# State part with the first Neumann matrices on GpSimd, and routed key chunks with products of 512 columns

## The chip, the core and the metric

The kernel runs on one core of a Trainium2 chip. A core has TensorE (matrix products into PSUM), VectorE, ScalarE and GpSimd (element-wise work), and SyncE, which issues the DMAs here. Each engine has its own queue and runs it in order; they wait for each other by semaphores. The metric is the time of one execution on the device in microseconds (us), the median of several. The profile is of one execution, and its own time stands beside the median below.

## What is computed

Two layers over 256 tokens of width 1024, all in float32. The first is an attention and pooling block with a gated FFN. The second is a Conformer-like convolution beside an RWKV-7 recurrence, followed by a PEER layer (product keys, 16,384 experts). The change touches the recurrence part and the PEER keys:

```python
def conformer_conv(p_conv, w_dw, b_dw, ln_w, ln_b):
    a, b = jnp.split(p_conv, 2, axis=-1)
    y = a * jax.nn.sigmoid(b)
    y = lax.conv_general_dilated(y, w_dw[:, None, :], ..., feature_group_count=CONV_CH) + b_dw   # 31 taps, 512 channels
    mu = jnp.mean(yf, axis=-1, keepdims=True)
    var = jnp.mean(jnp.square(yf - mu), axis=-1, keepdims=True)
    yf = (yf - mu) * lax.rsqrt(var + LN_EPS) * ln_w + ln_b
    return jax.nn.silu(yf)

def step(state, inp):                       # rwkv7_mix, scanned over 256 tokens, 8 heads of 64
    r_t, k_t, v_t, w_t, kk_t, a_t = inp
    sa = jnp.einsum('bhij,bhj->bhi', state, -kk_t)
    state = state * w_t + sa[..., None] * (kk_t * a_t) + v_t[..., None] * k_t
    y_t = jnp.einsum('bhij,bhj->bhi', state, r_t)
    return state, y_t

def chunk(xc):                              # peer_ffn
    ... the 16 best of 128 x 128 experts of each of 8 heads, gate = softmax(best)
    h = jax.nn.gelu(jnp.einsum('thkd,td->thk', ue, xc), approximate=False)
    return jnp.einsum('thk,thkd->td', (gate * h).astype(xc.dtype), ve)
```

## The kernel before

**Weights.** All weight matrices come as chunks of 128x1024 float32 (512 KB) through a ring of four slots (`RING`): SyncE loads `raw`, ScalarE writes its rounded copy `w_hi` (`split`, L497), and VectorE subtracts to get the rest, `w_lo` (`split`, L926). In the W_Q stage and the first chunks of the key table GpSimd does that subtraction (`lo_part`, L1540). The activations are split in the same way into `x_hi` and `x_lo`. TensorE then makes three products for each of 8 tiles of a chunk (`three`, L1576 to L1578: w_hi x_hi, w_hi x_lo, w_lo x_hi), 24 matmuls of 256 columns. `chunk_used` frees the ring slot.

**State part** (about 516 to 614 us). The recurrence is computed in four blocks of 64 tokens. First come the Gram products of the features (L1900), masked on VectorE (L1259, `gram_masked`); VectorE then adds the identity to the four masked matrices `DU` and so makes `R` (L1264, `neu_start`). Ten Neumann steps (list `NEUMANN`, products at L1920 to L1924, all 64x64) follow, each over four blocks, in one queue of 40 jobs on TensorE. A job waits until all results of the job three before it are evicted: by ScalarE (L771, `neu_act`) or by VectorE (`neu_dve`). A step's product that is evicted by ScalarE is a plain copy. Then come `m1` (L1938), `w1` (L1942), `m1T` (L1949), `m2` (L1955), `phi` (L1965), `u` (L1974 and L1975), the state chain of two steps (L1982, each with VectorE work between), `sa` (L1990) and the outputs `y` (L2008, L2022).

The 31-tap convolution runs beside it. Eleven taps are VectorE's own (`own_tap`, L1243, placed between its evictions). Twenty are made in 40 halves: ScalarE multiplies (`tap_pair`, L750, two operations of 128x256, into a buffer of three halves, so half m waits for the addition of half m - 3), and GpSimd adds each to `co` (L1565, 128x512). ScalarE makes 8 of the 40 ahead of the steps, 24 after evictions of the steps, 4 after `m1T` and 4 after `m2`. After the state chain, VectorE adds both sums (`conv_out`) and computes the bonus (`bonus_gate`); TensorE sums for the LayerNorm's mean (`ln_mean`, L1996) and variance (`ln_var`, L2013).

**Key table** (EXP_U, 128 chunks, 655 to 1126 us). From chunk 60 on (`DENSE_AT`) each chunk also does one of 64 groups of routing: VectorE makes one-hot matrices (`hots`, L1447), ScalarE multiplies gates in (`gates_in`, L856), TensorE makes `dense` products (L2071), VectorE multiplies them with stored activations (`mix`, L1459 and L1461; `late`, L1470). ScalarE applies gelu (`h_step`, L846 and L848). Key chunks use bank n % 4. **Value table** (EXP_V, 128 chunks, `v_step`, L2105): 512-column products, operands `f_hi`, `f_lo` (L1485) for the first chunk.

The order on each engine is the order in which the code is written; no scheduler moves it.

Of the kernel before, what the change touches and what calls it, by code (L numbers as in the profile page):

```python
# [26 lines left out]
P = 128  # L27
TOK = 256
# [113 lines left out]
ACT_TAPS = 20  # L142

# [27 lines left out]
def build(nc, ins, out):  # L171
    with ExitStack() as ctx:
# [17 lines left out]
        x_hi = sb("x_hi", [P, KT, TOK], F32R)  # L190
        x_lo = sb("x_lo", [P, KT, TOK], F32R)
# [201 lines left out]
        gT = i0T  # L393

# [91 lines left out]
        def _(act):  # L486
# [294 lines left out]
            while pair < 2 * ACT_TAPS - 4:  # L781
                tap_pair(pair)
                pair += 1
# [3 lines left out]
            while pair < 2 * ACT_TAPS:  # L787
                tap_pair(pair)
                pair += 1
# [5 lines left out]
            act.activation(rstd2, bank[1][:, 0:TOK], ACT.Sqrt, bias=V("eps", 1, 2), scale=1.0 / 512).then_inc(S("ln_std"), 1)  # L795
            for f in range(2):
                act.wait_ge(S("y_prod"), 2)
                act.activation(yy.rearrange("p f (t c s) -> p c f t s", t=2, c=2)[:, f], bank[4 * f][:, :].rearrange("p (f t s) -> p f t s", f=4, t=2),
                               ACT.Copy).then_inc(S("y_out"), 1)
# [39 lines left out]
            def h_step(n):  # L839

                if n <= DENSE_AT:
                    split(EXP_U + n + AHEAD)
                act.wait_ge(chunk_used, EXP_U + n + 1)
# [6 lines left out]
                if DENSE_AT <= n < NKEY - 1:  # L850
                    split(EXP_U + n + AHEAD + 1)
# [7 lines left out]
            for n in range(NKEY):  # L859
                if n == EXP_AT:  # L860
                    act.wait_ge(S("best_shifted"), 1)
                    act.activation(gate[:, :, :, :], gate[:, :, :, :], ACT.Exp).then_inc(S("gate_exp"), 1)
                if n == DENSE_AT:
                    act.wait_ge(S("gT"), 1)
# [3 lines left out]
                if n == NKEY - 1:  # L868
                    act.wait_ge(S("g_mixed"), GROUPS)
                    act.activation(by_four(f_hi[:, :]), h_chunk(0), ACT.Copy).then_inc(S("g_hi"), 1)  # L870
                h_step(n)
# [43 lines left out]
        def _(dve):  # L915
# [288 lines left out]
            dve.sem_inc(S("rk"), 1)  # L1204
# [9 lines left out]
            dve.sem_inc(S("factors"), 1)  # L1214
# [17 lines left out]
            dve.sem_inc(S("bonus_read"), 1)  # L1232
# [30 lines left out]
            for b in range(4):  # L1263
                dve.tensor_tensor(R_[:, b], DU[:, b], mask("eye64"), ALU.add).then_inc(S("neu_start"), 1)  # L1264
# [24 lines left out]

            for t in range(2):  # L1290
# [5 lines left out]

            for c in range(4):
# [4 lines left out]

            def decay_of(c):
# [6 lines left out]
            own.after(dve.memset(st[:, 0], 0.0))  # L1310

# [14 lines left out]
            dve.wait_ge(S("tap_added"), 2 * ACT_TAPS)  # L1326
            for f in range(2):
                v = slice(2 * f, 2 * f + 2)
                dve.wait_ge(S("own_taps"), 4 * (31 - ACT_TAPS))
                own.mark(dve.tensor_tensor(co[:, v], bank[6 + f][:, :].rearrange("p (a t) -> p a t", a=2), co[:, v], ALU.add))  # L1330
            own.wait()
            dve.sem_inc(S("conv_out"), 1)
            for f in range(4):
                bonus_gate(f)
            own.wait()
            dve.wait_ge(S("ln_mean"), 1)
            for f in range(4):
                dve.scalar_tensor_tensor(co[:, f], bank[1][:, 0:TOK], -1.0 / 512, co[:, f], ALU.mult, ALU.add).then_inc(S("ln_centred"), 1)
            for n in range(19, 22):
                split(MIX + n + AHEAD)  # L1340
# [4 lines left out]

            for f in range(2):
# [50 lines left out]
            dve.sem_inc(S("best_shifted"), 1)  # L1397
# [36 lines left out]
            dve.sem_inc(S("gate_done"), 1)  # L1434
# [4 lines left out]
            dve.tensor_copy(gT[:, :], bank[5][:, 0:TOK]).then_inc(S("gT"), 1)  # L1439
# [782 lines left out]
```

## Time and profile before

| | us |
|---|---|
| median of 3 runs (1490.42 to 1492.27) | 1491.6 |
| the profiled execution | 1492.93 |
| its span | 1491.1 |
| TensorE busy | 1419.8 (95%) |
| VectorE busy | 1043.9 (70%) |
| ScalarE busy | 824.2 (55%) |
| GpSimd busy | 190.4 (13%) |

Times are from the start of the span. PE is TensorE, PEld its weight load, DVE is VectorE, ACT is ScalarE, POOL is GpSimd.
### The profile page before, as it was taken

Reading aid. Unit: us, or ns where it says so; the run is one execution under the profiler, and the core shown is the slowest. Engines: PE = TensorE matmul, PEld = TensorE weight load, DVE = VectorE, ACT = ScalarE, POOL = GpSimd, SP = SyncE. Lnnn points to the kernel's source line nnn. Section 1 sums busy time; section 2 is a strip of 40 time slices with the busy share of each in tenths; the row PEclk is TensorE's granted clock in tenths of the full one; section 3 lists DMA queues with packets and bytes.
Section 4 is the critical chain, followed back from the end, with each engine's and each line's share of the span. In section 5 each row is a group of like instructions: output and inputs, shape, how many; then the busy total and the mean of one; then the engine's idle time right before and its main releaser. Section 6 shows DMA issues by size and latency. Waiting matters only on the chain.

```text
span 1491.1 us, 30993 instructions
## 1 busy us (share of the span) xinstructions
PE 1419.8 (95%) x11674; PEld 1328.9 (89%) x11674; DVE 1043.9 (70%) x1848; ACT 824.2 (55%) x1548; POOL 190.4 (13%) x108
## 2 busy tenths in 40 slices
PE   5999899999979987889999999999999999999997
PEld 5989889999969987889999999999998888888885
DVE  5478657878767685569973978889985555555554
ACT  6344546656547773545444567777765545544553
POOL 0030000000000272047884000000000000000000
PEclk9999999999999997999999999999999999999999
DMA  6547556667734300354555554444446555555551
GB/s 238 191 153 256 186 198 212 241 229 267 253 102 139 100 4 4 114 183 157 185 183 189 179 168 138 138 139 141 142 143 218 191 195 193 191 194 196 189 192 56
DMA packets 68372, 253.00 MB, mean 170 GB/s; under 512 B 7584, under 2 KB 7840, under 8 KB 67488
## 3 DMA queue, kind: packets, MB, share of 16 engines
q1 hardware_dynamic: 67104, 245.40, 48.5%
q10 hardware_dynamic: 1152, 5.98, 1.0%
q8 instruction: 82, 1.34, 0.4%
q14 instruction: 34, 0.28, 0.1%
HBM read 249.25 MB, written 2.10 MB: 169 GB/s over the span
## 4 chain that ended last, share of the span: by engine, by line
PE 89%; DVE 5%; ACT 3%; issue 2%; POOL 1%; DMA 0%; ACTq 0%; DVEq 0%; POOLq 0%
PE bank L2105 23%; PE bank L1576 18%; PE bank L1577 18%; PE bank L1578 18%; PE bank L2071 4%; PE bank L1924 1%; DVE arena L947 1%; POOL arena L1565 1%; PE bank L2056 0%; DVE arena L944 0%; PE bank L1619 0%; PE bank L1634 0%; DVE w_lo L926 0%; DMA vec<-in_vec 0%; PE bank L1843 0%
## 5 line engine op out<-in xcount | busy, mean ns | idle before, releaser
L1576 PE MATMUL bank<-x_hi,w_hi 128*128 128x256 f32 x2120 | 620.2, 293 | 17.9 <-DVE x_lo L957 6.3
L926 DVE TENSOR_TENSOR w_lo<-raw,w_hi 128x1024 fp32r<-128x1024 f32 x364 | 445.2, 1224 | 228.8 <-ACT w_hi L497 225.9
L1578 PE MATMUL bank<-x_hi,w_lo 128*128 128x256 f32 x2120 | 604.5, 285 | 0.0
L1577 PE MATMUL bank<-x_lo,w_hi 128*128 128x256 f32 x2120 | 604.5, 285 | 0.0
L497 ACT ACTIVATE w_hi<-raw 128x1024 fp32r<-128x1024 f32 x416 | 439.0, 1056 | 182.7 <-PE bank L2105 167.2
L1576 PEld LDWEIGHTS bank<-x_hi,w_hi 128*128 128x128 f32 x2120 | 411.1, 194 | 28.3 <-issue 20.7
L1577 PEld LDWEIGHTS bank<-x_lo,w_hi 128*128 128x128 f32 x2120 | 412.1, 194 | 0.4
L1578 PEld LDWEIGHTS bank<-x_hi,w_lo 128*128 128x128 f32 x2120 | 411.1, 194 | 0.0
L2105 PE MATMUL bank<-w_hi,x_lo 128*128 128x512 f32 x508 | 156.5, 389 | 0.0
L2105 PE MATMUL bank<-w_lo,x_hi 128*128 128x512 f32 x508 | 156.4, 389 | 0.0
L2105 PE MATMUL bank<-w_hi,x_hi 128*128 128x512 f32 x508 | 156.3, 389 | 0.0
L1540 POOL TENSOR_TENSOR w_lo<-raw,w_hi 128x1024 fp32r<-128x1024 f32 x52 | 125.6, 2416 | 100.3 <-ACT w_hi L497 100.3
L2105 PEld LDWEIGHTS bank<-w_hi,x_lo 128*128 128x128 f32 x508 | 95.3, 188 | 19.9
L2105 PEld LDWEIGHTS bank<-w_hi,x_hi 128*128 128x128 f32 x508 | 95.3, 188 | 19.8
L2105 PEld LDWEIGHTS bank<-w_lo,x_hi 128*128 128x128 f32 x508 | 95.3, 188 | 19.7
L856 ACT ACTIVATE xres<-xres,i0T 128x128 f32<-128x128 f32 x256 | 81.9, 391 | 47.7 <-DVE xres L1447 47.7
L1565 POOL TENSOR_TENSOR arena<-arena 128x512 f32<-128x512 f32 x40 | 50.3, 1288 | 431.5 <-ACT arena L750 431.5
L848 ACT ACTIVATE arena<-bank 128x256 f32<-128x256 f32 (+32 forms) x123 | 40.4, 328 | 89.0 <-PE bank L1578 89.0
L1447 DVE TENSOR_TENSOR xres<-kept,bank 128x1024 f32<-128x1024 f32 x64 | 78.1, 1221 | 16.4 <-PE bank L2071 16.3
L2071 PE MATMUL bank<-xres 128*128 128x128 f32 x512 | 67.6, 275 | 0.0
L2071 PEld LDWEIGHTS bank<-xres 128*128 128x128 f32 x512 | 62.8, 192 | 0.0
L1576 PE MATMUL bank<-f_hi,w_hi 128*128 128x256 f32 x184 | 53.1, 288 | 2.5 <-DVE f_lo L1122 2.5
(316 smaller groups left out, 1488.1 us busy)
## 6 DMA issues: line engine op xcount, KB each, us to landing
raw<-in_u SPq DMA_DIRECT2D x128, 512.0 KB, 3.2
raw<-in_v SPq DMA_DIRECT2D x128, 512.0 KB, 4.3
raw<-in_w_in SPq DMA_DIRECT2D x54, 512.0 KB, 4.3
arena<-in_ada SPq DMA_DIRECT2D x48, 512.0 KB, 5.0
raw<-in_w_up SPq DMA_DIRECT2D x44, 512.0 KB, 4.9
raw<-in_w_down SPq DMA_DIRECT2D x22, 512.0 KB, 3.7
raw<-in_w_out SPq DMA_DIRECT2D x16, 512.0 KB, 4.3
raw<-in_w_q SPq DMA_DIRECT2D x16, 512.0 KB, 3.2
```

Of the source, the lines that this page charges most:

```text
L497: act.activation(w_hi[:, s], raw[:, s], ACT.Copy).then_inc(hi_ready, 1)
L848: m = act.activation(h_chunk(n)[:, built // 4:], by_four(b[:, built:TOK]), ACT.Gelu)
L856: m = act.activation(hot[:, g % 2, 0, k], hot[:, g % 2, 0, k], ACT.Copy, scale=gT[:, 4 * g + k:4 * g + k + 1])
L926: dve.tensor_tensor(w_lo[:, s], raw[:, s], w_hi[:, s].bitcast(F32), ALU.subtract).then_inc(lo_ready, 1)
L1447: dve.tensor_tensor(hot[:, g % 2], iota.rearrange("p (c k s) -> p c k s", c=1, k=1).broadcast_to([P, 2, 4, 128]), e, ALU.is_equal)\
L1540: pool.tensor_tensor(w_lo[:, b % RING], raw[:, b % RING], w_hi[:, b % RING].bitcast(F32), ALU.subtract)\
L1565: pool.tensor_tensor(co[:, v], co[:, v], tap_product[:, 2 * (m % 3):2 * (m % 3) + 2], ALU.add).then_inc(S("tap_added"), 1)
L1576: pe.matmul(o, w, xh, start=start, stop=False, skip_group_check=True)
L1577: pe.matmul(o, w, xl, start=False, stop=False, skip_group_check=True)
L1578: return pe.matmul(o, wl, xh, start=False, stop=stop_, skip_group_check=True)
L2071: m = pe.matmul(bank[6 + g % 2][:, k * P:k * P + P], hot[:, g % 2, 0, k], hot[:, g % 2, 1, k], start=True, stop=True)
L2105: m = pe.matmul(bank[4 + 2 * a + half][:, :], left, right[:, s, half * 512:half * 512 + 512], start=begins, stop=ends, skip_group_check=True)
```

## The change

In the state part:
- The four `R = DU + eye` additions (128x256) move from VectorE to GpSimd, behind its 6th tap addition.
- ScalarE makes 32 tap halves after evictions of the Neumann steps instead of 24; none is left after `m1T` and `m2`.
- VectorE adds the two convolution sums ahead of its `m1` copies, and does `bonus_gate` ahead of `phi`. TensorE's `ln_mean` goes right behind `phi`, `ln_var` behind `u`, ahead of the state chain; both use bank 6. The rest of the LayerNorm follows the `sa` additions, and the three low parts that stood in it now stand behind it. The outputs `y` use banks 0 and 1.

In the key table, for chunks 60 to 126:
- `x_hi` and `x_lo` lie side by side (`x_pair`), and a tile takes one product of 512 columns with `w_hi` and one of 256 with `w_lo`: 16 matmuls a chunk instead of 24.
- The bank's right half (w_hi x_lo) is copied to SBUF by ScalarE (`right_half`), and VectorE adds it to the left half (`add_right`), before gelu.
- The low parts of these chunks (from chunk 64 of the key table to the second of the value table) are made by GpSimd instead of VectorE.

Some semaphores are merged into `mixer_made` and `gate_made`.

```diff
@@ ScalarE @@
-                        if pair < 2 * ACT_TAPS - 8 and (s, b) != (9, 3):
+                        if pair < 2 * ACT_TAPS:
                             tap_pair(pair)
                             pair += 1
...
-            while pair < 2 * ACT_TAPS - 4:
-                tap_pair(pair)
-                pair += 1
...
-            while pair < 2 * ACT_TAPS:
-                tap_pair(pair)
-                pair += 1
+            assert pair == 2 * ACT_TAPS
...
             def h_step(n):
 
-                if n <= DENSE_AT:
+                if n < DENSE_AT:
                     split(EXP_U + n + AHEAD)
-                act.wait_ge(chunk_used, EXP_U + n + 1)
+                if paired(n):
+                    act.wait_ge(S("u_added"), n - DENSE_AT + 1)
+                else:
+                    act.wait_ge(chunk_used, EXP_U + n + 1)
...
-                if DENSE_AT <= n < NKEY - 1:
-                    split(EXP_U + n + AHEAD + 1)
+
+            def right_half(n):
+
+                act.wait_ge(chunk_used, EXP_U + n + 1)
+                if n > DENSE_AT:
+                    act.wait_ge(S("u_added"), n - DENSE_AT)
+                act.activation(right, bank[n % RING][:, TOK:2 * TOK], ACT.Copy).then_inc(S("u_right"), 1)
...
+                if paired(n):
+                    right_half(n)
+                    split(EXP_U + n + AHEAD + 1)
                 h_step(n)
@@ VectorE @@
-            for b in range(4):
-                dve.tensor_tensor(R_[:, b], DU[:, b], mask("eye64"), ALU.add).then_inc(S("neu_start"), 1)
...
+            def add_right(n):
+
+                dve.wait_ge(S("u_right"), n - DENSE_AT + 1)
+                b = bank[n % RING]
+                dve.tensor_tensor(b[:, 0:TOK], b[:, 0:TOK], right, ALU.add).then_inc(S("u_added"), 1)
+
             for n in range(DENSE_AT, NKEY):
                 g = n - DENSE_AT
+                if paired(n):
+                    add_right(n)
                 if g + 2 < GROUPS:
                     hots(g + 2)
...
                 late(n)
-                if n < NKEY - 1:
-                    split(EXP_U + n + AHEAD + 1)
+            dve.wait_ge(lo_ready, EXP_V + AHEAD)
@@ GpSimd @@
                 pool.tensor_tensor(co[:, v], co[:, v], tap_product[:, 2 * (m % 3):2 * (m % 3) + 2], ALU.add).then_inc(S("tap_added"), 1)
+                if m == 5:
+                    eye = C("eye64").rearrange("p (a s) -> p a s", a=1).broadcast_to([P, 4, 64])
+                    for b in range(4):
+                        pool.wait_ge(S("gram_masked"), b + 1)
+                        pool.tensor_tensor(R_[:, b], DU[:, b], eye, ALU.add).then_inc(S("neu_start"), 1)
...
+            first = EXP_U + DENSE_AT + AHEAD + 1
+            pool.wait_ge(lo_ready, first)
+            with pool.Fori(0, (NKEY - DENSE_AT - 1) // RING) as i:
+                for p in range(RING):
+                    lo_part(first + p, i)
+            for b in range(first + (NKEY - DENSE_AT - 1) // RING * RING, EXP_V + AHEAD):
+                lo_part(b)
@@ TensorE @@
+            def reduce_pair(b, o):
+
+                s = b % RING
+                pe.wait_ge(lo_ready, b + 1)
+                for k in range(KT):
+                    c = slice(k * P, k * P + P)
+                    pe.matmul(o[:, :], w_hi[:, s, c], x_pair[:, k].rearrange("p a t -> p (a t)"), start=k == 0, stop=False, skip_group_check=True)
+                    m = pe.matmul(o[:, 0:TOK], w_lo[:, s, c], x_hi[:, k], start=False, stop=k == KT - 1, skip_group_check=True)
                 m.then_inc(chunk_used, 1)
...
+            pe.wait_ge(S("mixer_made"), CONV_OUT_AT)
+            for f in range(4):
+                m = pe.matmul(bank[6][:, 0:TOK], ones, co[:, f], start=f == 0, stop=f == 3)
+            m.then_inc(S("ln_mean"), 1)
...
             pe.wait_ge(S("phi"), 4)
+            pe.wait_ge(S("ln_sq"), 4)
+            for f in range(4):
+                m = pe.matmul(bank[6][:, 0:TOK], ones, cy[:, f, 0:TOK], start=f == 0, stop=f == 3)
+            m.then_inc(S("ln_var"), 1)
```

GpSimd, from the pooling of the first layer to the end of the taps, before and after (L1565 is the tap addition, L1585 after the change; L1590 the addition of the identity):

```order
L1548 TENSOR_TENSOR arena<-arena 128x2x265
L1549 TENSOR_TENSOR arena<-arena 128x257
L1552 TENSOR_TENSOR arena<-arena 128x256 x4
L1555 TENSOR_TENSOR arena<-arena 128x256 x4
L1565 TENSOR_TENSOR arena<-arena 128x512 x40
L1568 UNCONDITIONAL_BRANCH
```

```order
L1568 TENSOR_TENSOR arena<-arena 128x2x265
L1569 TENSOR_TENSOR arena<-arena 128x257
L1572 TENSOR_TENSOR arena<-arena 128x256 x4
L1575 TENSOR_TENSOR arena<-arena 128x256 x4
L1585 TENSOR_TENSOR arena<-arena 128x512 x6
L1590 TENSOR_TENSOR arena<-arena 128x256 x4
L1585 TENSOR_TENSOR arena<-arena 128x512 x34
L1593 UNCONDITIONAL_BRANCH
```

Four additions of 128x256 now stand between the 6th and the 7th of the 40 tap additions.

TensorE, end of the state part, before: the chain (L1982), `sa`, `ln_mean`, first `y`, `ln_var`, second `y`.

```order
L1982 MATMUL bank<-arena 64x64 x16
L1990 MATMUL bank<-arena 64x64 x32
L1996 MATMUL bank<-arena,kept 128x256 x4
L2008 MATMUL bank<-arena 64x64 x32
L2013 MATMUL bank<-arena,kept 128x256 x4
L2022 MATMUL bank<-arena 64x64 x64
L2026 MATMUL bank<-arena 128x256 x4
```

And after, from `ln_var` (L2027) on; `ln_mean` (L2011) now stands ahead of all of this, between `phi` and `u`:

```order
L2027 MATMUL bank<-arena,kept 128x256 x4
L2033 MATMUL bank<-arena 64x64 x16
L2041 MATMUL bank<-arena 64x64 x32
L2054 MATMUL bank<-arena 64x64 x32
L2064 MATMUL bank<-arena 64x64 x64
L2068 MATMUL bank<-arena 128x256 x4
```

The two sums of 128 rows have left the products behind the chain.

## Rows read from the trace of the kernel before

**Rows 1.** The page's first line.

```profile
span 1491.1 us, 30993 instructions
```

**Rows 2.** Chain that ended last, key and value tables: start, us, engine, out, line, operations.

```profile
876.37 0.89 PE bank L2071 x8
...
1113.67 0.89 PE bank L2071 x8
...
1126.21 348.47 PE bank L2105 x1536
```

**Rows 3.** Busy times in the routed key chunks: stretch, length, then each engine.

```profile
core 0: us, PE busy (x) PEld busy (x) DVE busy (x) ACT busy (x) POOL busy (x), PEclk, DMA share, GB/s
880.00:1113.00 233.00, 233.00 (x1982) 233.00 (x1981) 209.20 (x374) 165.09 (x434) 0.00 (x0) 1.00 0.42 142
```

**Rows 4.** Timeline of ScalarE, first Neumann steps.

```profile
519.45 0.38 ACT L771 ACTIVATE arena<-bank 128x256 f32<-128x256 f32 x1 [0.77 <-PE bank L1924]
...
520.79 0.90 ACT L750 ACTIVATE arena<-arena,vec 128x256 f32<-128x256 f32 x2
```

**Rows 5.** Timeline of ScalarE, one routed key chunk.

```profile
904.92 1.28 ACT L856 ACTIVATE xres<-xres,i0T 128x128 f32<-128x128 f32 x4 [0.76 <-DVE xres L1447]
```

**Rows 6.** Groups of GpSimd by form: busy us, mean ns, idle before.

```profile
L1540 POOL TENSOR_TENSOR w_lo<-raw,w_hi 128x1024 fp32r<-128x1024 f32 x52 | 125.6, 2416 | 100.3 <-ACT w_hi L497 100.3
L1565 POOL TENSOR_TENSOR arena<-arena 128x512 f32<-128x512 f32 x40 | 50.3, 1288 | 431.5 <-ACT arena L750 431.5
L1555 POOL TENSOR_TENSOR arena<-arena 128x256 f32<-128x256 f32 x4 | 4.8, 1218 | 0.1
L1552 POOL TENSOR_TENSOR arena<-arena 128x256 f32<-128x256 f32 x4 | 3.4, 876 | 0.1
```

**Rows 7.** Timeline of VectorE, end of the key table.

```profile
1125.74 0.42 DVE L1485 TENSOR_TENSOR f_lo<-arena,f_hi 128x256 fp32r<-128x256 f32 x1
```

**Rows 8.** Timeline of VectorE, start of the Neumann steps.

```profile
521.46 5.63 DVE L1264 TENSOR_TENSOR arena<-arena 128x256 f32<-128x256 f32 x4
```

**Rows 9.** Timeline of GpSimd, Neumann steps.

```profile
516.37 30.31 POOL L1565 TENSOR_TENSOR arena<-arena 128x512 f32<-128x512 f32 x24 [1.07 <-ACT arena L750]
```

**Rows 10.** Timeline of TensorE, first jobs of the Neumann steps.

```profile
518.72 3.95 PE L1924 MATMUL bank<-arena 64*64 64x64 f32 x128 [1.24 <-DVEq L1262]
523.18 1.15 PE L1924 MATMUL bank<-arena 64*64 64x64 f32 x32 [0.51 <-ACT arena L771]
...
528.16 1.15 PE L1924 MATMUL bank<-arena 64*64 64x64 f32 x32 [1.67 <-ACT arena L771]
529.57 1.81 PE L1924 MATMUL bank<-arena 64*64 64x64 f32 x45 [0.27 <-ACT arena L771]
```

**Rows 11.** Busy times around gaps of TensorE; columns as in rows 3.

```profile
413.90:416.20 2.30, 0.00 (x0) 0.00 (x0) 1.82 (x4) 0.86 (x2) 0.00 (x0) 0.99 0.67 230
416.30:419.50 3.20, 3.20 (x15) 3.20 (x16) 1.22 (x1) 1.88 (x3) 0.00 (x0) 0.50 0.66 192
...
570.60:572.30 1.70, 0.00 (x0) 0.00 (x0) 1.12 (x4) 1.70 (x5) 1.70 (x2) 1.00 0.04 10
573.30:577.70 4.40, 4.40 (x105) 4.40 (x101) 0.42 (x1) 2.41 (x6) 4.40 (x5) 0.50 0.00 0
573.30:593.60 20.30, 14.36 (x224) 12.44 (x222) 10.50 (x27) 2.41 (x6) 5.58 (x5) 0.50 0.00 1
```

**Rows 12.** Timeline of TensorE, end of the state part.

```profile
561.86 2.08 PE L1938 MATMUL bank<-arena 64*64 64x64 f32 x64 [0.48 <-ACT arena L771]
...
579.85 1.12 PE L1982 MATMUL bank<-arena 64*64 64x64 f32 x16 [1.87 <-DVE arena L1312]
...
588.76 3.78 PE L1996 MATMUL bank<-arena,kept 128*128 128x256 f32 x8 [2.11 <-DVEq L1332]
...
597.50 2.74 PE L2022 MATMUL bank<-arena 64*64 64x64 f32 x128
```

More of the change, by code:

```diff
@@ L393, in build, with paired @@
         gT = i0T
+        def paired(n):
+            return DENSE_AT <= n < NKEY - 1
+        right = vec[:, 0:TOK]
+        assert COL["final_g_2"] >= TOK
         def v_pair(n):
@@ L1288, in _ @@
             assert taps == 4 * (30 - ACT_TAPS)
+            dve.wait_ge(S("tap_added"), 2 * ACT_TAPS)
+            for f in range(2):
+                v = slice(2 * f, 2 * f + 2)
+                dve.wait_ge(S("own_taps"), 4 * (31 - ACT_TAPS))
+                own.mark(dve.tensor_tensor(co[:, v], bank[6 + f][:, :].rearrange("p (a t) -> p a t", a=2), co[:, v], ALU.add))
+            own.wait()
+            dve.sem_inc(S("mixer_made"), 1)
             for t in range(2):
@@ L1301, in _ @@
                    .then_inc(S("phi"), 1)
+            dve.wait_ge(S("ln_mean"), 1)
+            for f in range(4):
+                dve.scalar_tensor_tensor(co[:, f], bank[6][:, 0:TOK], -1.0 / 512, co[:, f], ALU.mult, ALU.add).then_inc(S("ln_centred"), 1)
             def decay_of(c):
@@ L1309, in _ @@
                 own.mark(dve.tensor_tensor(u0[:, c], src, decay_of(c), ALU.mult))
-            own.after(dve.memset(st[:, 0], 0.0))
+            own.wait()
             dve.tensor_copy(st[:, 1], u0[:, 0]).then_inc(S("state"), 1)
@@ L1324, in _ @@
                        .then_inc(S("sa"), 1)
[L1326 to L1340, printed above, removed]
             dve.wait_ge(S("ln_std"), 1)
@@ L1344, in _ @@
                 dve.tensor_tensor(co[:, f], co[:, f], rstd2, ALU.mult).then_inc(S("ln_y"), 1)
+            for n in range(19, 22):
+                split(MIX + n + AHEAD)
             for f in range(2):
@@ L1977, in _ @@
             pe.wait_ge(S("phi"), 4)
+            pe.wait_ge(S("ln_sq"), 4)
+            for f in range(4):
+                m = pe.matmul(bank[6][:, 0:TOK], ones, cy[:, f, 0:TOK], start=f == 0, stop=f == 3)
+            m.then_inc(S("ln_var"), 1)
             for c in range(1, 3):
@@ L1993, in _ @@
                     m.then_inc(S("sa_prod"), 1)
-            pe.wait_ge(S("conv_out"), 1)
-            for f in range(4):
-                m = pe.matmul(bank[1][:, 0:TOK], ones, co[:, f], start=f == 0, stop=f == 3)
-            m.then_inc(S("ln_mean"), 1)
             def y_place(h, t, c):
                 f, r = h // 2, HALF[h % 2]
-                return bank[4 * c][r, f * P + t * 64:f * P + t * 64 + 64]
+                return bank[c][r, f * P + t * 64:f * P + t * 64 + 64]
             for h in range(8):
@@ L2010, in _ @@
             m.then_inc(S("y_prod"), 1)
-            pe.wait_ge(S("ln_sq"), 4)
-            for f in range(4):
-                m = pe.matmul(bank[1][:, 0:TOK], ones, cy[:, f, 0:TOK], start=f == 0, stop=f == 3)
-            m.then_inc(S("ln_var"), 1)
             pe.wait_ge(S("y_prod"), 1)
```

45 lines of the change are left out of this document (28 added, 17 removed).

## The prediction, made before the result was known

> **What bounds the kernel now.** I began with the first line of the page [rows 1]: the span is 1491.1 us and the profiled execution took 1492.9, which is 1.3 us over the median of 1491.6. All sums below are made on the profiled execution, and 1.3 is taken off at the end.
>
> Next I read the chain that ended last. In the routed half of the key table it is one engine: a group of `dense` products comes every (1113.67 - 876.37) / 63 = 3.767 us, and nothing but matmuls lies between two of them [rows 2]. Of a period the dense products are 0.89, so the 24 matmuls of a chunk (256 columns each) are 2.87 us, 119.7 ns each. In the value table that follows, 1536 matmuls of 512 columns took 348.47 us, 226.9 ns each. The table of busy times says the same: TensorE 233.0 of 233 us, VectorE 209, ScalarE 165, GpSimd nothing [rows 3]. Only fewer or cheaper matmuls shorten this stage; what VectorE gives up there is worth nothing.
>
> The state part (516 to 600 us) is different. TensorE does small 64x64 products, and waits for evictions and for the other engines. There the question is who is late, and at which clock TensorE runs.
>
> **The routed key chunks.** 67 chunks (n = 60 to 126) get 8 products of 512 columns and 8 of 256, where there were 24 of 256: 8 x (226.9 + 119.7) ns = 2.773 us for 2.873. That is 0.10 us less per chunk, 6.7 us in all. From below, if a 512-column product cost just two of 256 (239.4 ns), the gain is nothing. From above I have no row in which 512 columns are cheaper than 226.9. The rows of the value table are of the same data type and size, so I take them. The Trainium skill ("TensorE: Matmul & The Clock Gate", section "Back-to-back issue gap") gives an isolated product of N columns N/2.4 + 2.5 ns: one of 512 would save only 2.5 ns against two of 256, an estimated 1.3 us over 67 chunks. Rows 2 show 12.5 ns, five times that, and the measurement decides.
>
> What hides the rest: ScalarE gets one more copy of 128x256 per chunk. The nearest row, an eviction of that size, has 0.38 us [rows 4], so its 165.09 / 233 x 3.767 = 2.67 become 3.05 us of a period of 3.67. Its tightest wait now is for VectorE's one-hot matrices [rows 5], 0.76 us a period, so some 0.3 us are left. VectorE loses a low part of 1.22 and gains an addition of 0.42: from 3.38 down to 2.6. GpSimd takes a low part in 2.416 us [rows 6], below 3.67 and below 2.77, so it keeps up. A bank comes round only after four chunks, so the longer way (right half, addition, gelu) is covered by three chunks, some 10 us. If that cover were gone, the period would grow by what the slowest engine lacks; that is a rival below.
>
> One new wait stands at the end. The first low half of the value stage, `f_lo`, takes 0.42 us on VectorE at 1125.74 [rows 7], reading two SBUF operands. Such operations seem to stand still while GpSimd runs one: the four additions of L1264 took 5.63 us, 1.41 each, with GpSimd at work beside them [rows 8], where `f_lo`, of equal size, took 0.42 with GpSimd idle. GpSimd's last low part (2.416) now lies around `f_lo`, and the value stage waits for it. From 0 to 2.4 us; I take half, 1.2. **Routing: 1.2 - 6.7 = -5.5 us.**
>
> **The four eye additions move to GpSimd.** They were VectorE's 5.63 us [rows 8], which held only taps of its own. On GpSimd they stand behind the 6th tap addition. Prices there: 1288 ns for 512 columns and 2416 for 1024 [rows 6]; the line through both gives 0.72 for 256 columns, and the two rows of 256 have 0.88 and 1.22. So four of them take 2.9 us (2.6 to 4.9), I take the line since it is of plain additions in a full queue.
>
> GpSimd's tap additions are back to back there, 24 in 30.31 us, 1.26 each [rows 9], the first of the 24 being the 5th. The 6th ends at 516.37 + 2.53 = 518.9, the eyes at 521.8, the 7th addition at 523.1, the 8th at 524.3. Who waits: ScalarE alternates evictions and tap pairs in one queue, and a pair waits for an addition two back, since its product buffer holds three. Pair 9, behind the 2nd eviction, waits for the 7th addition (before, it went at 520.79 [rows 4]). So the 3rd eviction starts at 524.0, the next pair waits for the 8th addition, and the 4th eviction starts at 525.3. TensorE's 4th job ends at 518.72 + 3.95 = 522.67, and its 5th waits for the 3rd and 4th eviction: 525.8 in place of 523.18 [rows 10]. **TensorE then has no matmul for 3.1 us** (2.8 to 5), where it had 0.5. The two jobs after it keep gaps of about 1.3, as now. The third step begins at 533.7 in place of 530.8.
>
> **What 3 us of silence do to TensorE's clock.** The granted clock of the windows is 0.99 in the 2.3 us without a matmul at 413.9, and 0.50 (1.2 GHz) while it works from 416.3 to 419.5; likewise at 570.6 and 573.3 [rows 11]. Seven stretches of 1.8 us or more without a matmul at full clock are in this trace, the first at 85.8 and the last at 640.3, and each was followed by half clock within 3.6 us. The gap of 1.67 before 528.16 was not: 32 records took 1.15 us there, as before it [rows 10]. So a gap of 3.1 us should be followed by the 1.2 GHz level.
>
> How long does it last? Where 128-row products followed (416.3), some 3.2 us. Where 64x64 products followed (573.3), it lasted 20.3 us [rows 11], though TensorE was busy without a break for the first 4.4. It came back 4.9 us after the first 128-row product, `ln_mean` at 588.76 [rows 12]. The Neumann steps are all 64x64. So I take it that the clock stays at half from about 528 to the first 128-row product. The Trainium skill (same page, section "What's actually happening") says that activity releases the throttle. By that alone it would be back some microseconds after the gap; 573.3 to 577.7, busy and still at 0.50, speaks against it for 64x64. It is rival 2.
>
> The price. At full clock, (3.95 - 1.15) / 96 = 29.2 ns a record; at half, 16 records took 1.12 with some 0.27 of it a single record's length, 53.5 ns [rows 10, 12]. From the third step to `m1` there are 56 products of 16 records, 896. Before, 530.8 to 561.86. After, TensorE itself is the bound: 533.7 + 896 x 53.5 ns + 0.4 for the last eviction = 582.0, or +20.1.
>
> **The tail.** `m1` to `phi` are 320 records, 17.1 us, to 599.1. Then the moved `ln_mean` at 3.8 (its row was at half as well), to 602.9, and the clock returns about 604. `u`: 128 records, 4.2, to 607.1; `ln_var` 1.9, to 609.0; the state chain 3.3 (full clock, two turns through VectorE), `sa` 1.7, `y` 1.8 and 2.7: 618.5. Before, the last `y` product ended at 597.50 + 2.74 = 600.24 [rows 12]. So **+18.3 us**. Without the clock's fall the tail is where the change gains: the taps are all done by `m1`, so the gap of 1.9 before the chain, the gap of 2.1 before `ln_mean`, and the half clock that covers them go.
>
> **Forecast (0.60).** 1492.9 + 18.3 - 5.5 - 1.3 = 1504.4, rounded to 1504.5. Its own range is 1494 (clock falls a step late or comes back a little earlier, routing gains all 6.7) to 1511 (longer eyes, `u` wholly at half, routing gains 1).
>
> **Rival 1 (0.15): the clock holds**, because the gap is shorter than I make it or TensorE's next work saves it. The products end 2.5 us later than now, 564.4; `phi` 573.1, `ln_mean` 575.0, `u` 578.7, `ln_var` 580.6, chain 583.9, the `y` products 590.1: 10.1 earlier. 1492.9 - 10.1 - 5.5 - 1.3 = 1476.0. If the clock falls only around the chain, 1481.
>
> **Rival 2 (0.13): the clock falls, and returns in the second or third step**, since TensorE has no gap from there on. The steps have slack against the other engines at full clock (26.2 us of records in 31), which takes most of the loss back: +1, so 1477.
>
> **Rival 3 (0.05): it returns midway**, each microsecond of half clock costing about 0.4: 1481 to 1497.
>
> **Rival 4 (0.07): ScalarE or VectorE bounds the routed loop.** From 0.6 us more per chunk on ScalarE than I count, the period exceeds 3.67; at 3.9 it is 64 x 0.23 = 15 us over my routing term. With half clock 1519; with full clock 1491. For it: the longer way for each chunk. Against it: 0.6 us of idle time left on ScalarE, 1 on VectorE.
>
> **Chances and range.** Faster by over 0.2% (3 us, about what a measurement of this kernel tells from none) is rivals 1 and 2 and part of 3: 0.30. Within it: 0.04. Slower, the forecast and most of rival 4: 0.66. The sign is split, so the range of eight in ten takes in both sides: 1475 to 1511.
>
> **What the profile after would show.** Half clock from about 528 to 603, 16 records in 0.86 us and not in 0.47, VectorE and ScalarE waiting on TensorE throughout; a gap of about 3 us on TensorE before its 5th job; four operations of about 0.72 us on GpSimd between tap additions; a period of 3.67 from dense group to dense group; a gap of about 1 us ahead of the first value product. I am wrong if the 5th job waits under 1.8 us, or if the granted clock is 1.00 from 535 on.

## The result, and the profile after

The changed kernel took 1478.1 us (median of six runs, 1475.9 to 1480.6) where the kernel before took 1490.8 in the same comparison: a ratio of 0.9916, interval 0.9902 to 0.993. It is 12.7 us **faster**; 1504.5, slower, was forecast. Its profiled execution took 1480.5. The first line of the page:

```profile
span 1478.6 us, 30218 instructions
```

Parts of the chain that ended last (start, length, what):

```profile
868.10 0.89 PE bank L2113 x8
...
1100.22 0.89 PE bank L2113 x8
...
1113.76 348.47 PE bank L2150 x1536
```

Against [rows 2], the first dense group comes 8.3 us earlier (868.10 for 876.37), the value table 12.45 (1113.76 for 1126.21): so some 8.3 us are from the state part and 4.2 from the routed chunks. The timeline of TensorE, which answers to [rows 10] and [rows 12]:

```profile
518.64 3.95 PE L1966 MATMUL bank<-arena 64*64 64x64 f32 x128 [1.24 <-DVEq L1278]
525.34 1.97 PE L1966 MATMUL bank<-arena 64*64 64x64 f32 x32 [2.75 <-ACT arena L779]
527.79 1.98 PE L1966 MATMUL bank<-arena 64*64 64x64 f32 x32 [0.48 <-ACT arena L779]
...
563.56 2.08 PE L1980 MATMUL bank<-arena 64*64 64x64 f32 x64 [0.48 <-ACT arena L779]
...
572.17 1.99 PE L2011 MATMUL bank<-arena,kept 128*128 128x256 f32 x8
...
577.65 1.99 PE L2027 MATMUL bank<-arena,kept 128*128 128x256 f32 x8
...
588.22 2.74 PE L2064 MATMUL bank<-arena 64*64 64x64 f32 x128
```

The gap ahead of the 5th job is there, 2.75 us, and the two jobs behind it take 1.97 where they took 1.15. But `m1` starts at 563.56, and both 128-row sums (L2011, L2027) take 1.99 where `ln_mean` took 3.78. Busy times, columns as in rows 3:

```profile
523.00:525.00 2.00, 0.00 (x0) 0.00 (x0) 0.03 (x1) 1.95 (x6) 2.00 (x2) 1.00 0.00 0
525.00:528.40 3.40, 2.58 (x44) 2.45 (x46) 0.82 (x2) 3.24 (x9) 3.40 (x4) 0.50 0.00 0
528.40:531.80 3.40, 2.92 (x55) 2.76 (x54) 1.22 (x4) 3.25 (x10) 3.40 (x4) 0.50 0.02 5
531.90:535.30 3.40, 3.32 (x107) 3.13 (x105) 2.15 (x6) 3.22 (x9) 3.40 (x4) 1.00 0.00 0
```

The clock fell to 1.2 GHz at 525.0 and was at 2.4 again from 531.9, with nothing but 64x64 products in between. That is what my forecast excluded. The gap arises as worked out: four additions on GpSimd, and behind them a tap pair of ScalarE that waits for GpSimd (a run below tests it):

```profile
518.75 2.79 POOL L1590 TENSOR_TENSOR arena<-arena 128x256 f32<-128x256 f32 x4
...
522.80 0.91 ACT L758 ACTIVATE arena<-arena,vec 128x256 f32<-128x256 f32 x2 [1.98 <-POOL arena L1585]
```

At the start of the value table `f_lo` takes 2.10 us beside GpSimd's last low part, where [rows 7] has 0.42, and TensorE waits 1.30:

```profile
1111.61 2.10 DVE L1506 TENSOR_TENSOR f_lo<-arena,f_hi 128x256 fp32r<-128x256 f32 x1
...
1113.76 0.73 PE L2150 MATMUL bank<-w_hi,f_hi 128*128 128x512 f32 x2 [1.30 <-DVE f_lo L1506]
```

Two open questions follow. Why did 64x64 products bring the clock back at 531.9, and not after 573.3 in the kernel before [rows 11]? And which parts of the change earn the 12.7 us?

One thing on comparing runs. The clock also falls after gaps early in the kernel, for about 3.4 us in one execution and 6.8 in the next, whatever the kernel, and this moves all that follows by some 2 us. The first Neumann job (L1924 before) starts at 518.72 in one profiled execution and at 516.42 in another. So for the state part I count from the start of that job. `m1` is at +43.1 before and at +44.9 after; the last `y` product ends at +81.5 before and at +72.3 after, 9.2 us less.

### The profile page after: what moved, and what is told of

Same layout as the page of the kernel before. It is cut to its first block, busy times and chain, and to the rows that moved or that the text cites. A ratio compares the mean times of both kernels' runs of the same rounds, so it can differ in the third digit from the quotient of the medians.

```text
span 1478.6 us, 30218 instructions
## 1 busy us (share of the span) xinstructions
PE 1413.0 (96%) x11138; PEld 1300.3 (88%) x11138; DVE 993.4 (67%) x1844; ACT 844.6 (57%) x1615; POOL 354.1 (24%) x179
## 4 chain that ended last, share of the span: by engine, by line
PE 88%; DVE 5%; ACT 3%; issue 2%; POOL 1%; DMA 0%; ACTq 0%; DVEq 0%; POOLq 0%
PE bank L2150 24%; PE bank L1608 14%; PE bank L1609 13%; PE bank L1610 13%; PE bank L1627 8%; PE bank L1628 4%; PE bank L2113 4%; PE bank L1966 1%; ACT w_hi L505 1%; DVE w_lo L942 1%; POOL arena L1585 1%; DVE arena L963 1%; PE bank L2098 0%; DVE arena L960 0%; PE bank L1661 0%
## 5 line engine op out<-in xcount | busy, mean ns | idle before, releaser
L1608 PE MATMUL bank<-x_pair,w_hi 128*128 128x256 f32 x1584 | 464.1, 293 | 16.4 <-DVE x_pair L970 5.5
L1609 PE MATMUL bank<-x_pair,w_hi 128*128 128x256 f32 x1584 | 453.8, 286 | 0.0
L1610 PE MATMUL bank<-x_pair,w_lo 128*128 128x256 f32 x1584 | 453.5, 286 | 0.0
L1560 POOL TENSOR_TENSOR w_lo<-raw,w_hi 128x1024 fp32r<-128x1024 f32 x119 | 286.3, 2406 | 263.6 <-ACT w_hi L505 189.6
L1608 PEld LDWEIGHTS bank<-x_pair,w_hi 128*128 128x128 f32 x1584 | 308.9, 195 | 26.7 <-issue 20.5
L1609 PEld LDWEIGHTS bank<-x_pair,w_hi 128*128 128x128 f32 x1584 | 310.1, 196 | 0.4
L1610 PEld LDWEIGHTS bank<-x_pair,w_lo 128*128 128x128 f32 x1584 | 309.6, 195 | 0.0
L2150 PE MATMUL bank<-w_hi,x_pair 128*128 128x512 f32 x1016 | 271.7, 389 | 0.0
L2150 PEld LDWEIGHTS bank<-w_hi,x_pair 128*128 128x128 f32 x1016 | 190.7, 188 | 39.5
L1627 PE MATMUL bank<-x_pair,w_hi 128*128 128x512 f32 x536 | 195.4, 404 | 0.0
L2150 PE MATMUL bank<-w_lo,x_pair 128*128 128x512 f32 x508 | 156.4, 389 | 0.0
L1628 PE MATMUL bank<-x_pair,w_lo 128*128 128x256 f32 x536 | 149.8, 279 | 0.0
L1585 POOL TENSOR_TENSOR arena<-arena 128x512 f32<-128x512 f32 x40 | 49.6, 1270 | 411.5 <-ACT arena L758 411.5
L1627 PEld LDWEIGHTS bank<-x_pair,w_hi 128*128 128x128 f32 x536 | 100.8, 188 | 20.7
L2150 PEld LDWEIGHTS bank<-w_lo,x_pair 128*128 128x128 f32 x508 | 95.3, 188 | 19.9
L1628 PEld LDWEIGHTS bank<-x_pair,w_lo 128*128 128x128 f32 x536 | 101.2, 189 | 0.0
```

The costliest lines, as they stand in the source:

```text
L1560: pool.tensor_tensor(w_lo[:, b % RING], raw[:, b % RING], w_hi[:, b % RING].bitcast(F32), ALU.subtract)\
L1585: pool.tensor_tensor(co[:, v], co[:, v], tap_product[:, 2 * (m % 3):2 * (m % 3) + 2], ALU.add).then_inc(S("tap_added"), 1)
L1608: pe.matmul(o, w, xh, start=start, stop=False, skip_group_check=True)
L1609: pe.matmul(o, w, xl, start=False, stop=False, skip_group_check=True)
L1610: return pe.matmul(o, wl, xh, start=False, stop=stop_, skip_group_check=True)
L1627: pe.matmul(o[:, :], w_hi[:, s, c], x_pair[:, k].rearrange("p a t -> p (a t)"), start=k == 0, stop=False, skip_group_check=True)
```

## The experiments

**The identity additions back on VectorE.** The four `R` additions stand on VectorE again, where they were.

```diff
-                if m == 5:
-                    ... four pool.tensor_tensor(R_[:, b], DU[:, b], eye, ALU.add)
+            for b in range(4):
+                dve.tensor_tensor(R_[:, b], DU[:, b], mask("eye64"), ALU.add).then_inc(S("neu_start"), 1)
```

> The changed kernel with its four identity additions back on VectorE, all else as changed. Theory A (read from the two traces): the gap of 2.75 us before TensorE's 5th job comes from these additions standing between two tap additions on GpSimd; it drops the clock, which comes back 6.9 us later, and the loss of 1.7 us at m1 is all that is left of it. Then no gap here is over 1.7 us, the clock stays at 1.00 from 516 to 562, m1 starts at 561.8 instead of 563.6, and the time is 1.7 us under the changed kernel, about 1476.4. Rival: m1 is late because of the eight more tap pairs between the evictions, not because of the clock: then m1 stays at 563.5 and the time too. VectorE's additions take 5.6 us again, 1.4 each.

Measured: 1475.1 us (1474.9 to 1476.4), ratio to before 0.9888 (0.9871 to 0.9904). The timeline of TensorE:

```profile
516.42 3.95 PE L1963 MATMUL bank<-arena 64*64 64x64 f32 x128 [1.24 <-DVEq L1278]
520.88 1.15 PE L1963 MATMUL bank<-arena 64*64 64x64 f32 x32 [0.51 <-ACT arena L779]
...
525.85 4.00 PE L1963 MATMUL bank<-arena 64*64 64x64 f32 x77 [1.67 <-ACT arena L779]
...
559.36 2.08 PE L1977 MATMUL bank<-arena 64*64 64x64 f32 x64 [0.48 <-ACT arena L779]
```

`m1` is at +42.9, 2.0 earlier than in the changed kernel, with all the tap pairs still in the steps. So the additions on GpSimd cost the 2 us, not the pairs. The last `y` product ends at +68.95, 3.4 earlier than in the changed kernel (+72.32): the other 1.4 us come behind `m1`, where the changed kernel had half clock from 583.1 to 586.5 and this execution had none. The expectation that the clock would not fall was wrong: it was at half from 526.1 to 529.6, behind a gap of 1.67 us. In the kernel before, the same gap left it at full.

```profile
526.20:529.50 3.30, 3.30 (x69) 3.30 (x66) 3.12 (x9) 3.19 (x9) 3.30 (x3) 0.50 0.02 5
529.70:533.00 3.30, 3.18 (x118) 3.08 (x114) 2.46 (x6) 3.19 (x9) 3.30 (x3) 1.00 0.02 5
```

It came back once more under 64x64 products, and this fall cost nothing at `m1`: the steps have slack.

**GpSimd's identity additions made twice.** A second loop of the same four additions, so that the gap is longer.

> The changed kernel with GpSimd making its four identity additions twice over. TensorE's gap before its 5th job grows from 2.75 to about 5.6 us. If the time that the clock stays down depends on the gap, it is down for longer than 6.9 us this time; if on what TensorE does afterwards, it is down some 3.4 to 10 us again and comes back under the same 64x64 products. m1 starts 2 to 3 us later than the changed kernel's 563.6, and the time is 2 to 3 us over it: the steps' slack was used up by the first gap. By the recorded forecast's reasoning half clock would last to the mean's products in both.

Measured: 1482.2 us in one run. The gap was 5.60 us, `m1` at 566.31 (+47.8, 2.8 later than in the changed kernel).

```profile
528.10 1.97 PE L1969 MATMUL bank<-arena 64*64 64x64 f32 x32 [5.60 <-ACT arena L779]
...
566.31 2.08 PE L1983 MATMUL bank<-arena 64*64 64x64 f32 x64 [0.48 <-ACT arena L779]
```

The clock was down from 525.2 to 532.0, as long as with the gap of 2.75, though the gap itself covers the first 2.9 us of it. So in this pair of runs its length did not follow the length of the gap. The 2.85 us added to the gap came through to `m1` in full: the steps' slack was used up.

**The state part alone.** The changed state part with the routed chunks as before.

```diff
         def paired(n):
-            return DENSE_AT <= n < NKEY - 1
+            return False
```

(with the low parts back on VectorE, and ScalarE's split behind its gelu, which the diff above leaves out)

> The state part as changed, the routed key chunks as before (24 products of 256 columns, low parts on VectorE, no copy of a right half). From the two traces: the first routed group comes 8.3 us earlier than before, the first value product then 8.3 us earlier too, not 12.4: time about 8.3 under before, 1482.5. If the routing part gave nothing but moved its gain from somewhere else, it would be at the changed kernel's time, 1478. The period from dense group to dense group is 3.767 us again instead of 3.684.

Measured: 1484.3 us (1484.1 to 1485.0), ratio 0.9948 (0.9931 to 0.9964), 8.4 under before. The period from dense group to dense group is 3.767 us again, as expected, and `f_lo` takes 0.43 us again. So the state part gives 8 us and the routing the remaining 4 or so, as the traces divide them.

**Only the tap pairs moved.** The kernel before with one line changed.

```diff
-                        if pair < 2 * ACT_TAPS - 8 and (s, b) != (9, 3):
+                        if pair < 2 * ACT_TAPS:
```

> The kernel before with one edit: all 32 remaining tap halves are made between the evictions of the Neumann steps, none behind m1T and m2. Theory G (the gap of 1.80 us before the u products, in which ScalarE makes taps ahead of the m2 copies, is what drops the clock at 573.2): the gap goes, the clock stays at full, u, the chain, sa and the mean run at full speed and the state part is about 7 us shorter, 1485.5. Rival: the gaps of 1.9 and 2.1 us around the chain drop it all the same: 1.5 to 3 us shorter, 1489 to 1491. Neither expects the full 8.3 of the changed kernel's state part, since the mean is still waited for behind sa.

Measured: 1489.0 us against 1491.4, ratio 0.9985 (0.9975 to 0.9994). The timeline of TensorE:

```profile
576.24 1.40 PE L1982 MATMUL bank<-arena 64*64 64x64 f32 x16 [1.87 <-DVE arena L1312]
...
585.42 3.78 PE L1996 MATMUL bank<-arena,kept 128*128 128x256 f32 x8 [2.11 <-DVEq L1332]
...
594.09 2.74 PE L2022 MATMUL bank<-arena 64*64 64x64 f32 x128
```

The gap before `u` went, and the clock did not fall there. It fell at 576.5 instead, behind the gap of 1.87 ahead of the chain, and stayed at half to 590.1, so that `ln_mean` still took 3.78. The last `y` product ends at +78.2: the pairs alone give 3.3 of the state part's 9.2 us. The other 5.9 came only with the rest of the change. I put them down to the moved sums, which set two times 1.99 us of 128-row work around `u` and take the gap of 2.11 out; no run has the sums moved alone, so that share is argued and not measured. In time this is the rival of the expectation (1489 to 1491).

**The halves of a Neumann product apart.** Now the open question on the clock. A 64x64 product reads one of the two partition halves. In the steps the halves alternate from product to product; in `u` 16 products in a row read the same half. First the steps, with their two inner loops exchanged:

```diff
-                        for u in range(4):
-                            for c, rc in enumerate(HALF):
+                        for c, rc in enumerate(HALF):
+                            for u in range(4):
```

> The changed kernel with the two loops inside a Neumann product exchanged: four products of one partition half, then four of the other, where now they alternate. Theory P: the clock came back at 531.9 under 64x64 products since these alternate the halves; the u products of the kernel before, which stay in one half for 16 products and came with half clock from 573.3 to 577.7, do not. By P the clock stays at half much longer here, up to the first 128-row product at worst: m1 at up to 582, time up to 18 us over the changed kernel. Theory U: the order of the halves is nothing to the clock, what held it down in the kernel before was the waiting between 578 and 588.8. By U the clock is back at about 532 again and m1 starts at 563.6.

Measured: 1481.7 us in one run. Busy times and the first job:

```profile
526.60:533.30 6.70, 6.36 (x99) 6.20 (x99) 2.46 (x6) 6.40 (x18) 6.70 (x7) 0.50 0.01 2
```

```profile
516.76 4.99 PE L1966 MATMUL bank<-arena 64*64 64x64 f32 x128 [1.24 <-DVEq L1278]
```

Half clock from 526.5 to 533.4, 6.9 us again, `m1` at +49.3. The products in runs of four are slower at full clock too: the first 128 records take 4.99 us where they took 3.95. By this run alone theory P fell.

**`u` with alternating halves.** The kernel before with the same 64 products of `u` in another order.

```diff
-            for c in range(4):
-                t, r = c // 2, slice(64 * (c % 2), 64 * (c % 2) + 64)
-                for h in range(8):
...
+            for t in range(2):
+                for h in range(8):
...
+                    for left, right in ((bt, m2), (kt_, vt)):
+                        for c, r in enumerate(HALF):
...
```

> The kernel before with the u products alternating the two partition halves (blocks 0 and 1 interleaved, then 2 and 3), 64 products as before. Theory P (the order of the halves decides whether 64x64 products bring the clock back): it falls at about 573.2 and is back at about 580, 6.9 us later, so that the mean's products take 1.9 instead of 3.78 us, and the state part is some 3 to 5 us shorter. Theory U (the waiting between 578 and 588.8 holds it down): half clock until 593.7 as before, no more than 1 us of difference.

Measured: 1492.0 us in one run, no clear difference. `u` itself took 3.15 us instead of 5.63, but the chain waited longer for VectorE (2.48 for 1.87), and half clock lasted from 573.2 to 590.3. The last `y` product ended at +79.4, 2.1 us less than before, between what the two theories expect. `u` is over at 575.5 here, too short to show whether it would have brought the clock back. So I made it longer.

**`u` three times over, order as before.**

```diff
-            for c in range(4):
...
+            for again in range(3):
+                for c in range(4):
...
```

> The kernel before with the 64 u products made three times over, the result the same: TensorE is then busy with them without a break for some 12 to 17 us from 572.4 on, where it had 5.6. Theory U (what holds the clock down after 573.2 is the waiting from 578 on): the clock is back at about 580 or earlier, 3.4 to 6.9 us after the fall, while u products run, and the last ones take 29 ns a record. Theory P (these products, which stay in one partition half for 16 at a time, do not bring it back however long they run): half clock through all of them, 384 records in about 20 us, until the 128-row products of the mean.

Measured: 1500.9 us in one run. The windows (PE and PEld busy, PEclk is the third number from the end):

```profile
571.00:575.00 4.00, 4.00 (x98) 4.00 (x96) 0.00 (x0) 1.87 (x5) 4.00 (x5) 0.50 0.01 4
575.00:579.00 4.00, 4.00 (x98) 4.00 (x96) 0.00 (x0) 0.00 (x0) 1.05 (x1) 0.50 0.00 0
579.00:585.00 6.00, 6.00 (x143) 6.00 (x139) 0.27 (x1) 0.00 (x0) 0.00 (x0) 0.50 0.01 3
```

The clock fell at 570.7 and stayed at half through 15 us in which TensorE was busy without a break, and further to 601.4. Waiting is not what held it down: theory U fell, and these products did not bring the clock back. Nor is it a lack of busy time or of products: the changed kernel's rows above have 44 and 55 records in 2.58 and 2.92 us of busy time in two half-clock stretches of 3.40, and the clock came back; here 98 records filled all 4.00 us of a stretch, and it did not.

**`u` three times over, alternating, and in runs of four.** First the alternating order from above with the loop of three around it. Then the half changed only after every four products, which is the diff shown.

```diff
+            for again in range(3):
+                for t in range(2):
+                    for pair in range(4):
+                        for c, r in enumerate(HALF):
+                            for h in (2 * pair, 2 * pair + 1):
...
```

> The kernel before with the u products three times over and alternating the partition halves from product to product. With one half for 16 products at a time, three times over, the clock stayed at half through all 16 us of them. Theory P (alternation brings it back): it falls about 1 us after they begin and returns 3.4 or 6.9 us later, while they still run or right behind them. Theory V (something else in the Neumann products brings it back): half clock until the mean's 128-row products.

> As the run before this one, but the half changes only after every four products (8 records), as in the Neumann steps with their halves apart, where the clock did come back after 6.9 us. If short runs are enough, the clock returns 3.4 or 6.9 us after its fall here too; they take 53 ns a record at half, so all 384 need up to 20 us. If it does not return, the difference between u and the steps is not the length of the runs.

Measured: 1493.9 and 1493.2 us in one run each. Alternating told nothing on the question: in that run the clock did not fall behind the gap of 1.80 (1.00 until 582.1), so there was nothing to come back from. In runs of four it fell at 571.0 and was back at 574.4, while the same products ran:

```profile
571.10:574.30 3.20, 3.20 (x133) 3.20 (x128) 0.00 (x0) 2.11 (x5) 3.20 (x4) 0.50 0.02 5
574.50:577.30 2.80, 2.80 (x190) 2.77 (x182) 0.00 (x0) 0.00 (x0) 1.91 (x2) 1.00 0.03 6
```

The operands and the number of products are those of the run that stayed at half for 15 us; only the order differs, runs of 4 for runs of 16.

**The steps in runs of eight.** The same tested where the forecast had placed it: in the changed kernel, all products of one half of a job first, runs of eight where a job has two products and of four where it has one.

```diff
-                    for k, (lhs, rhs, dst, how) in enumerate(step):
-                        for u in range(4):
-                            for c, rc in enumerate(HALF):
+                    for c, rc in enumerate(HALF):
+                        for k, (lhs, rhs, dst, how) in enumerate(step):
+                            for u in range(4):
...
-                        m.then_inc(S("neu_prod"), 1)
+                            if c:
+                                m.then_inc(S("neu_prod"), 1)
```

> The changed kernel with all products of one partition half of a Neumann job first, then those of the other: runs of 8 products where a job has two, 4 where it has one. The gap before the 5th job stays about 2.8 us or becomes smaller, since the first jobs take longer. If runs in one half are what kept half clock in the u products, it stays down longer than the 6.9 us seen with runs of four, perhaps to the first 128-row product (m1 up to 582). If not, it is back at about 533 and m1 is at 566 to 569, since products in runs take longer at full clock too (36 against 29 ns a record).

Measured: 1518.7 us in one run, some 41 over the changed kernel. Busy times, then the first jobs and the last of the steps:

```profile
523.00:528.00 5.00, 4.15 (x78) 3.93 (x77) 0.86 (x3) 4.80 (x13) 5.00 (x5) 1.00 0.00 0
529.00:535.00 6.00, 6.00 (x72) 6.00 (x70) 1.64 (x4) 5.55 (x14) 6.00 (x6) 0.50 0.01 3
540.00:560.00 20.00, 20.00 (x259) 20.00 (x259) 7.30 (x19) 8.22 (x21) 9.45 (x8) 0.50 0.01 2
```

```profile
518.66 6.42 PE L1966 MATMUL bank<-arena 64*64 64x64 f32 x128 [1.24 <-DVEq L1278]
525.35 1.87 PE L1966 MATMUL bank<-arena 64*64 64x64 f32 x32 [0.27 <-ACT arena L779]
527.80 2.43 PE L1966 MATMUL bank<-arena 64*64 64x64 f32 x29 [0.58 <-ACT arena L779]
...
595.87 6.50 PE L1966 MATMUL bank<-arena 64*64 64x64 f32 x125
602.85 2.08 PE L1981 MATMUL bank<-arena 64*64 64x64 f32 x64 [0.47 <-ACT arena L779]
```

The clock fell at 528.4, although no gap since the first job was longer than 0.58 us, and stayed at half for 72 us, to 600.1, with TensorE busy throughout. It returned in the last two steps, which have one product a job, so runs of four. Half clock through the steps, which the forecast gave the changed kernel, is what this one had, and from a cause that was not in the forecast: the order of the partition halves. Not all of the 41 us is the clock: at full clock the first 128 records already took 6.42 us where they took 3.95.

**Two repairs together, and a third.** The identity additions on VectorE; the last low part of the routed loop made by VectorE behind `f_lo`; then, in the second kernel, `u` alternating as well.

```diff
-            dve.wait_ge(lo_ready, EXP_V + AHEAD)
+            dve.wait_ge(lo_ready, EXP_V + AHEAD - 1)
+            split(EXP_V + AHEAD - 1)
...
-            for b in range(first + (NKEY - DENSE_AT - 1) // RING * RING, EXP_V + AHEAD):
+            for b in range(first + (NKEY - DENSE_AT - 1) // RING * RING, EXP_V + AHEAD - 1):
```

> The changed kernel with two edits: the identity additions back on VectorE, and the low part of the third value chunk made by VectorE, so that GpSimd no longer runs beside f_lo. Theory A: the value table starts 1.3 us earlier against the last key product (f_lo takes 0.42 instead of 2.10), on top of what the identity additions gave: 1475.1 - 1.3 = 1473.8. Rival: f_lo is early, but TensorE then waits for the low part of the second value chunk or for x_lo behind the subtraction that VectorE now makes: 1475.

> The changed kernel with identity additions and the last low part on VectorE, as measured together before (1474.6), and the u products alternating the partition halves from product to product. With halves in runs the 128 records of u take 3.6 us at full clock, 28 ns each; alternating, 258 records took 4.06, 15.7 ns each. So u is 1.6 us shorter, and what follows (the variance, the chain) comes 1.6 earlier: 1473.0. Rival: VectorE is then late with the centred mean and the squares, on which the variance waits, and at most 0.5 us is gained.

Measured: 1474.6 us (1471.8 to 1475.6), ratio 0.9883 (0.9862 to 0.9904); and 1474.3 (1472.8 to 1475.3), ratio 0.9881 (0.9862 to 0.99). In the trace of the first, VectorE and the chain:

```profile
1108.27 0.41 DVE L1508 TENSOR_TENSOR f_lo<-arena,f_hi 128x256 fp32r<-128x256 f32 x1
```

```profile
1096.88 0.89 PE bank L2111 x8
1109.12 348.20 PE bank L2148 x1536
```

From the last dense group to the value table it is 12.24 us, where the changed kernel has 1113.76 - 1100.22 = 13.54: the 1.3 us of the collision are gone. In the medians it is 0.5 us against the first repair alone (1475.1), within their spread. In the second, `u` took 2.24 us, but `ln_var` then waited 0.80 for ScalarE's squares; the last `y` product ends at +68.8 for +69.2, 0.4 us earlier, the rival of its expectation. By the medians the two are 3.5 and 3.8 us under the changed kernel. Nearly all of that is the first repair, which alone was 3.0 under it; what the other two add lies within the spread.

## Why the prediction was wrong

The step that failed is the sentence "So I take it that the clock stays at half from about 528 to the first 128-row product". It rested on one stretch, 573.3 to 577.7 in [rows 11], and read it as showing what 64x64 products do. The runs showed in its place that products of this size do both, by their order: under runs of 16 in one partition half the clock stayed at half (15 us, busy throughout), under runs of four of the same products it came back after 3.4 us, and under runs of eight in the steps it even fell. Each of these is one profiled execution. The Neumann steps alternate from product to product, and half clock ended after 3.4 to 6.9 us in all six profiled executions in which the clock fell while they ran in that order.

Point by point:

- **The gap**: 3.1 us forecast (2.8 to 5), 2.75 measured, just under the lower bound; four additions 2.9 forecast, 2.79 measured; the 5th job at 525.8 forecast, 525.34 measured. The path was right, and the run with the additions back on VectorE shows it.
- **The fall of the clock**: forecast from about 528, and it fell at 525.0. Right. The rule from seven gaps (1.8 us or more) is too sharp at its lower end. The trace that it was read from has an eighth fall, at 221.6, and the longest gap in the 30 us ahead of it is one of 1.45 at 217.7. Of nine profiled executions with the gap of 1.67, half clock followed in three, and one gap of 1.80 was not followed by it (`u` three times over, alternating).
- **Its price**: +20.1 at `m1` forecast, +1.8 measured; at the last `y` product +18.3 forecast, -9.2 measured. This one step is the miss, the half clock of the steps and that of `m1` to `ln_mean` behind them. The price of a record at half clock, 53.5 ns, was about right (32 records in 1.97 us, some 0.27 of it a single record's length), but only some 99 records of the steps ran at it, where the forecast had all 896 from the third step on.
- **The tail**: with the clock at full I had the last `y` product end at 590.1, in rival 1; it ended at 588.22 + 2.74 = 590.96, with half clock from 583.1 to 586.5. The size was about right. The run with only the tap pairs shows that the pairs alone do not give it; what the sums alone would give is not shown.
- **The routed chunks**: -5.5 forecast, -4.2 measured. The period is (1100.22 - 868.10) / 63 = 3.684, not 3.667: of 512 columns and 256 together 0.349, not 0.347. The wait at the value table was 1.3, forecast 1.2. Why a period takes 0.017 us more I did not settle. Of the Trainium skill's figure for the isolated product ("TensorE: Matmul & The Clock Gate", section "Back-to-back issue gap"), which would have given 1.3 us, the trace disagrees: 0.083 x 63 = 5.2 us were gained.
- **Rival 2**, 1477 with a chance of 0.13, describes what happened within 1.1 us: half clock ended in the second step. Part of the closeness is luck, since its sum has a routing gain 1.3 us too large and no second fall of the clock at 583.1. Its sentence from the Trainium skill (same page, "What's actually happening": activity releases the throttle) agrees with the steps (half clock from 525.0 to 531.9). I set it aside on the evidence of `u`; for `u` in its old order it does not hold (15 us busy at half clock).

What I should have done: `u` and the steps differ in their loops, which the code shows, and I compared them by tile size alone. With only one stretch to go by, 0.60 for the one outcome was too much.

## What to carry to other kernels

A stall of TensorE costs itself and the half clock behind it, and how long the latter lasts depended here on the products that followed: put 128-row products, or 64x64 products that change the partition half often, behind a wait, and keep long runs in one half away from it. Before a moved operation is put between others of a queue, follow who waits behind it: four additions of 0.7 us on GpSimd gave TensorE, two engines further, a wait of 2.75 us, of which 2.0 were left at `m1`. An operation on VectorE with two SBUF operands should not be placed beside GpSimd's last one, if TensorE waits for it (2.10 us for 0.42).

## What the runs showed of the hardware

- Order alone changes the speed of 64x64 products: at full clock 128 records of `u` took 3.62 us in runs of 16 (the changed kernel, 574.10 to 577.72) and 2.24 alternating (the last run above); the first 128 of the steps took 3.95 alternating, 4.99 in runs of four and 6.42 in runs of eight, all at full clock.
- Half clock can come without a long gap: in one run it did after 10 us of products in runs of eight with no gap above 0.58 us.
- Whether a gap of 1.67 or 1.80 us is followed by half clock differs between executions of the same stretch of code up to the gap.
- Why long runs in one half act so is not shown; only the order was varied. The half meant is that of the operands. In the steps a product writes the same half that it reads; in `u` the half that is written changes after every two products, also within a run. With the order of `u` the two PSUM banks of its results change more often too.
